# Banded attention scores in two matmul passes over stacked halves instead of three over zero-padded keys

## The reference

```python
q = q.reshape(B, nb, BLK, A_KV_HEADS, A_GROUP, A_HEAD_DIM) * (A_HEAD_DIM ** -0.5)   # 4 groups x 4 heads, 64 wide
kb = _band(k.reshape(B, S, A_KV_HEADS, A_HEAD_DIM), nb)      # keys of the blocks before, at and after
scores = jnp.einsum('bnqkgd,bnskd->bnkgqs', q, kb).astype(jnp.float32)
scores = scores - slopes * dist ; scores = where(|t-s| <= 128, scores, NEG)
p = softmax(concatenate([scores, sink]))[..., :-1]
out = jnp.einsum('bnkgqs,bnskd->bnqkgd', p, vb)
```

## Time and profile before

| | us |
|---|---|
| median of three runs | 1272.54 |
| lowest, highest | 1271.21, 1272.92 |
| span of the profiled execution (first to last instruction) | 1270.83 |
| TensorE matmuls busy | 1201.8 (95%) |
| VectorE busy | 634.5 (50%) |
| ScalarE busy | 370.1 (29%) |
| GpSimd busy | 432.6 (34%) |
| banded attention's groups: first score of g = 0, 1, 2, 3 at | 60.40, 97.33, 132.76, 168.87 |

### The profile page before, as it was taken

The page is one execution under the profiler, slowest core; times in us unless marked ns, Lnnn a source line. Parts: engine busy times, 40 slices in busy tenths (PEclk is TensorE's granted clock), DMA queues, the critical chain, the costliest instruction groups (busy, mean ns, idle before and its releaser), DMA issues.

```text
span 1270.8 us, 19309 instructions
## 1 busy us (share of the span) xinstructions
PE 1201.8 (95%) x5804; PEld 996.6 (78%) x5804; DVE 634.5 (50%) x1055; ACT 370.1 (29%) x719; POOL 432.6 (34%) x474
## 2 busy tenths in 40 slices
PE   6988899999999999999989899999999999999996
PEld 4777787878888888888967677777788888888885
DVE  6666674444432544445476767745433432343432
ACT  3167672232210011011165656532222200101101
POOL 5455543433321323334242314215333321333341
PEclk9999999999999999999999999999999999999998
DMA  6211012233333233332201001013323432333331
GB/s 158 67 35 33 17 34 67 84 99 99 90 109 98 85 98 89 106 114 88 76 18 36 19 17 33 1 34 116 99 83 99 117 93 80 92 98 99 109 90 66
DMA packets 176473, 96.62 MB, mean 76 GB/s; under 512 B 8753, under 2 KB 173105, under 8 KB 176433
## 3 DMA queue, kind: packets, MB, share of 16 engines
q1 hardware_dynamic: 176432, 96.12, 25.9%
HBM read 94.01 MB, written 2.10 MB: 76 GB/s over the span
## 4 chain that ended last, share of the span: by engine, by line
PE 78%; DVE 8%; issue 6%; POOL 3%; ACT 3%; DMA 1%; DVEq 0%; ACTq 0%; SPq 0%; POOLq 0%
PE bank L975 25%; PE bank L977 24%; PE bank L976 24%; PE bank L1419 2%; POOL w_hi L436 1%; PE bank L1116 1%; DVE stat L2010 1%; POOL bias L516 1%; DVE w_lo L1501 1%; DMA w_raw<-in_a_w_qkv 1%; DVE bpt_lo L2015 1%; DVE apt_lo L1672 0%; ACT s_b L906 0%; DVE k_dup L1592 0%; DVE w_lo L1518 0%
## 5 line engine op out<-in xcount | busy, mean ns | idle before, releaser
L1501 DVE TENSOR_TENSOR w_lo<-w_raw,w_hi 128x1024 fp32r<-128x1024 f32 (+2 forms) x151 | 202.9, 1344 | 294.5 <-POOL w_hi L436 294.4
L436 POOL TENSOR_SCALAR w_hi<-w_raw 128x1024 fp32r<-128x1024 f32 (+3 forms) x159 | 184.5, 1160 | 414.8 <-PE bank L977 404.3
L975 PE MATMUL bank<-x_hi,w_lo 128*128 128x512 f32 x784 | 309.2, 394 | 8.4 <-DVE w_lo L1501 5.3
L976 PE MATMUL bank<-x_lo,w_hi 128*128 128x512 f32 x784 | 306.9, 391 | 0.0
L977 PE MATMUL bank<-x_hi,w_hi 128*128 128x512 f32 x784 | 306.6, 391 | 0.0
L975 PEld LDWEIGHTS bank<-x_hi,w_lo 128*128 128x128 f32 x784 | 147.9, 189 | 41.6 <-DVE w_lo L1501 7.4
L977 PEld LDWEIGHTS bank<-x_hi,w_hi 128*128 128x128 f32 x784 | 148.2, 189 | 31.4
L976 PEld LDWEIGHTS bank<-x_lo,w_hi 128*128 128x128 f32 x784 | 148.2, 189 | 29.4
L975 PE MATMUL bank<-f_hi,w_lo 128*128 128x512 f32 x352 | 137.8, 391 | 1.1 <-DVE f_lo L1782 1.1
L977 PE MATMUL bank<-f_hi,w_hi 128*128 128x512 f32 x352 | 137.0, 389 | 0.0
L976 PE MATMUL bank<-f_lo,w_hi 128*128 128x512 f32 x352 | 137.0, 389 | 0.0
(11 more groups left out here) (215 smaller groups left out, 1946.9 us busy)
## 6 DMA issues: line engine op xcount, KB each, us to landing
w_raw<-in_ffn_w_gu SPq DMA_DIRECT2D x88, 512.0 KB, 3.8
w_raw<-in_ffn_w_down SPq DMA_DIRECT2D x32, 704.0 KB, 4.4
w_raw<-in_a_w_qkv SPq DMA_DIRECT2D x12, 512.0 KB, 3.7
w_raw<-in_a_w_o SPq DMA_DIRECT2D x8, 512.0 KB, 3.5
w_raw<-in_b_w_o SPq DMA_DIRECT2D x8, 512.0 KB, 3.8
w_raw<-in_b_w_in SPq DMA_DIRECT2D x4, 672.0 KB, 4.0
w_raw<-in_b_w_uq SPq DMA_DIRECT2D x4, 576.0 KB, 4.0
x_n<-in_x SPq DMA_DIRECT2D x4, 512.0 KB, 5.0
```

Of the source, the lines that this page charges most:

```text
L436: pool.tensor_scalar(split_part(w_hi, s, cols, kv), raw_part(s, cols, kv), 1.0, 1.0, ALU.mult, ALU.mult) \
L975: pe.matmul(o, ll, rh, start=start, stop=False)
L976: pe.matmul(o, lh, rl, start=False, stop=False)
L1501: dve.tensor_tensor(split_part(w_lo, s, cols, kv), raw_part(s, cols, kv), f(split_part(w_hi, s, cols, kv)), ALU.subtract) \
```

## The change

The queries are stacked instead of the keys being padded. `aq[:, hd]` has one 128-row tile for each head: the rounded query on the head's own 64 rows (0 to 63 for an even head, 64 to 127 for an odd one), and its remainder on the other 64 rows. `kp_hi` and `kp_lo` hold the group's keys twice, on both halves, with no zeros. One pass against `kp_lo` and one against `kp_hi` then sum all four partial products. The tiles that follow in memory keep their places (`k_rest` fills the room).

- PE: two matmuls for each score unit in place of three; the keys' and queries' semaphores count 1 and 4 for each group in place of 2 and 2.
- ACT: the rounding of a pair of heads (line 700) becomes two half-height operations, that of the keys (line 684) one full-height operation in place of two half-height ones.
- DVE: the remainders of a pair (line 1634) become two half-height operations that write the other half of the rows, each behind a wait of its own; the keys' remainder (line 1614) one in place of two. The zero fills of `kp_hi` and `kp_lo` at the start of the kernel (line 1559) go.

```diff
-                for b in range(2):
-                    act.activation(kp_hi[b * HD:(b + 1) * HD, b, :], k_dup[b * HD:(b + 1) * HD, g, :], ACT.Copy) \
-                        .then_inc(kp_hi_ready, 1)
+                act.activation(kp_hi[:], k_dup[:, g, :], ACT.Copy).then_inc(kp_hi_ready, 1)
...
                 wait(act, proj_free, U_Q + 2 * g + i + 1)
-                act.activation(aq_hi[:, i, :], q_tmp[:], ACT.Copy).then_inc(q_hi_ready, 1)
+                for odd in range(2):
+                    rows = slice(odd * HD, (odd + 1) * HD)
+                    act.activation(aq[rows, 2 * i + odd, :], q_tmp[rows, :], ACT.Copy).then_inc(q_hi_ready, 1)
...
-                    q = (slice(None), hd // 2, slice(n * P, (n + 1) * P))
-                    k = (slice(None), hd % 2, slice(k0 * P, (k0 + nk) * P))
-                    product(banks[u % 3][:, 0:nk * P], aq_hi[q], aq_lo[q], kp_hi[k], kp_lo[k], True, True) \
-                        .then_inc(s_done, 1)
+                    q = aq[:, hd, n * P:(n + 1) * P]
+                    k = slice(k0 * P, (k0 + nk) * P)
+                    pe.matmul(banks[u % 3][:, 0:nk * P], q, kp_lo[:, k], start=True, stop=False)
+                    pe.matmul(banks[u % 3][:, 0:nk * P], q, kp_hi[:, k], start=False, stop=True).then_inc(s_done, 1)
...
-                pe.wait_ge(kp_ready, 2 * g + 2)
-                pe.wait_ge(q_ready, 2 * g + 1)
+                pe.wait_ge(kp_ready, g + 1)
+                pe.wait_ge(q_ready, 4 * g + 2)
...
-                pe.wait_ge(q_ready, 2 * g + 2)
+                pe.wait_ge(q_ready, 4 * g + 4)
...
-            for t in (kp_hi, kp_lo, av_hi, av_lo):
+            for t in (av_hi, av_lo):
                 dve.memset(f(t[:]), 0.0).then_inc(vec_consts, 1)
...
-                for b in range(2):
-                    rows = slice(b * HD, (b + 1) * HD)
-                    wait(dve, kp_hi_ready, 2 * g + b + 1)
-                    dve.tensor_tensor(kp_lo[rows, b, :], k_dup[rows, g, :], f(kp_hi[rows, b, :]), ALU.subtract) \
-                        .then_inc(kp_ready, 1)
+                wait(dve, kp_hi_ready, g + 1)
+                dve.tensor_tensor(kp_lo[:], k_dup[:, g, :], f(kp_hi[:]), ALU.subtract).then_inc(kp_ready, 1)
...
-                wait(dve, q_hi_ready, 2 * g + i + 1)
-                dve.tensor_tensor(aq_lo[:, i, :], q_tmp[:], f(aq_hi[:, i, :]), ALU.subtract).then_inc(q_ready, 1)
+                for odd in range(2):
+                    rows, other = slice(odd * HD, (odd + 1) * HD), slice((1 - odd) * HD, (2 - odd) * HD)
+                    wait(dve, q_hi_ready, 4 * g + 2 * i + odd + 1)
+                    dve.tensor_tensor(aq[other, 2 * i + odd, :], q_tmp[rows, :], f(aq[rows, 2 * i + odd, :]),
+                                      ALU.subtract).then_inc(q_ready, 1)
```

More of the change, by code:

```diff
@@ L170, in build @@
             ("x_n", [P, NT, D], F32), ("sq0", [P, 2, T], F32), ("ss0", [P, T], F32)])
-        (q_tmp, aq_hi, aq_lo, k_dup, kp_hi, kp_lo, v_all, av_hi, av_lo, near, bias, s_a, apt_hi, apt_lo) = \
+        (q_tmp, aq, k_dup, kp_hi, kp_lo, _, v_all, av_hi, av_lo, near, bias, s_a, apt_hi, apt_lo) = \
             region(scratch, [
-                ("q_tmp", [P, T], F32), ("aq_hi", [P, 2, T], F32R), ("aq_lo", [P, 2, T], F32R),
-                ("k_dup", [P, GROUPS, T], F32), ("kp_hi", [P, 2, T], F32R), ("kp_lo", [P, 2, T], F32R),
+                ("q_tmp", [P, T], F32), ("aq", [P, HG, T], F32R),
+                ("k_dup", [P, GROUPS, T], F32), ("kp_hi", [P, T], F32R), ("kp_lo", [P, T], F32R),
+                ("k_rest", [P, 2, T], F32),
                 ("v_all", [P, NT, GROUPS * HD], F32),
@@ L498, in _ @@
             pool.wait_ge(pool_consts, 2 + HEADS)
-            pool.wait_ge(vec_consts, 6)
+            pool.wait_ge(vec_consts, 4)
             def a_group(g, last=False):
@@ L888, in _ @@
             b_q_hi(3, T_BPRE + 6)
-            act.wait_ge(vec_consts, 8)
+            act.wait_ge(vec_consts, 6)
             act.wait_ge(krope_pool, 4)
@@ L1055, in _ @@
                 k_block(k)
-            pe.wait_ge(vec_consts, 5)
+            pe.wait_ge(vec_consts, 3)
             pe.wait_ge(pt_free, KD)
@@ L1627, in a_q_out @@
                 if not (first and i == 0):
-                    wait(dve, q_ready, 2 * g + i)
+                    wait(dve, q_ready, 4 * g + 2 * i)
                 dve.scalar_tensor_tensor(q_tmp[:], banks[6 + i][:], HD ** -0.5, rs_t[:], ALU.mult, ALU.mult) \
@@ L1959, in b_k_lo @@
                 for b in range(2):
-                    wait(dve, kp_hi_ready, 2 * GROUPS + 4 * g + 2 * i + b + 1)
+                    wait(dve, kp_hi_ready, GROUPS + 4 * g + 2 * i + b + 1)
                     ins = dve.tensor_tensor(bk_lo[0:NOPE, 2 * i + b, :], banks[6 + i][b * HD:(b + 1) * HD, :],
```

## The result

The changed kernel takes 1278.67 us in the median of 7 executions (1275.49 to 1279.28), the kernel before 1272.92 (1271.14 to 1275.31) beside it. The ratio is 1.0039, 95% interval 1.0026 to 1.0052. The prediction was 1274.4 with a range up to 1277.0: the side was the one that its second rival named, the size is beyond all of its cases.

A forecast was written before the change was run, and what follows sets the result against it. The prediction took the chain over POOL, ACT and DVE, not PE, to bound most of each attention group. Borders 3 x 0.65 + 0.8 = 2.75 us added, 0.94 taken: +1.8 on 1272.5, rounded up to 1274.4; range 1270.8 to 1277.0.

The forecast's parts named there:

- What bounds the groups: Banded attention: PE bounds only the last 12.95 us of group 1; before that, a chain over POOL, ACT and DVE.
- rival 1: PE is the bound after all: all 9.3 us come off, less 2.75 at the borders, 1266 us; chance 8%.
- The savings on the chain: Unit 12 read one pass earlier per group, 0.48 us; unit 2 in group 3, 0.12; with unit 11's 0.34, 0.94 together.
- The further 0.34 for unit 11 at the low clock: Groups 0 and 2: a pass of unit 11 at clock 0.50 counts too, 0.34 us, or nothing if the clock stays up.
- ACT at the border: Borders of groups 0, 1 and 2: the second half-height rounding delays `ot_hi` and the bias, +0.65 us each group.
- DVE before group 3: Group 3: the second half-height remainder delays `ot_lo`, for which PE's output projection waits, +0.8 us, bounds 0.6 to 0.9.
- PE's wait for the second pair: Before unit 2, around 99.3 us in group 1: costs nothing, since unit 3 must wait beyond 100 anyway.
- The sum without falls: Borders add 2.75 us; the chain gives back 0.94, of which 0.34 only with the clock down in groups 0 and 2.
- The clock: Waits before unit 11 grow to about 2.4 us, PE idles more and may fall to 0.50; 25% for 1275.1 or more.
- 0.68 for a fall: Price of a clock fall in a group: group 2 with one lasted 36.11 us, group 1 without 35.43.
- the forecast's case: Borders cost more than the chain saves: 1274.4 us, itself from 1273.2 to 1275.1; chance 59%.
- rival 2: More clock falls around unit 11: one more gives +2.3 us, from the second +2.8, four +4.6 (1277); 25% for 1275.1 or more.

The follow-up runs named there:

- three medians: Changed kernel, fillers in group 0 alone: 1275.36 us; kernel before less one score pass, groups 0.92 longer: 1276.67; changed kernel, groups 0.92 longer: 1279.25.
- the fourth kernel: Changed kernel, odd half first on ACT and DVE, odd head's second rounding on POOL, no filler matmuls: 1275.14 us, ratio 1.0011.
- the two halves of the edit: Kernel before with one of three score passes left out: 1271.10 us; changed kernel with its pass against `kp_lo` made twice, so only borders differ: 1274.97.

## Right and wrong, step by step

- **What bounds the groups**: right. The part with full PE kept its 12.94 us, and 64 passes less, alone and with the clock held, are worth 0.56 us, where rival 1 wanted 9.3. The waits said so, the 95% did not.
- **The savings on the chain**: right in size, 0.56 measured for 0.60. The further 0.34 for unit 11 at the low clock rested on a fall that stays as it is; it did not.
- **ACT at the border**: the mechanism was right and the size too small. From the pair to `ot_hi` it is 0.70 for the 0.65 taken, inside the bounds. What the term had left out is that the hold goes on to the next operation: `av_hi` follows `ot_hi` after 0.41 in place of 0.28. Together 0.83, so 0.5 us more over three groups. The prediction had weighed the hold for DVE alone.
- **DVE before group 3**: right, 0.83 for 0.8. PE's wait for the second pair cost nothing, as said.
- **The sum without falls**: 2.75 - 0.60 = 2.15 by the prediction's terms; 2.7 by the profiles and 3.0 by the medians. ACT's term is 0.5 of the difference.
- **The clock**: this is the step that failed. The wait for unit 11 was expected at 2.4 us and came to 2.20; that it grows was seen, and that this side of the result hung on it too. But "0.68 for a fall" was read from groups with a fall of 3.4 us, the only kind in the attention of the trace of before, and taken as the price of any. What the forecast's case put at nothing, the 8.4 us of passes that turn into waits of PE, and rival 2 at 0.68 for each further fall, came to 4.2 us of falls by the fillers, where the kernel before had 1.2 to 1.5. The changed kernel's falls are twice as long, cost 1.5 to 1.7 each, and in the execution of the median they come in groups 0, 1 and 2; by their times nine of thirteen executions are like it. That one long fall moves the next group under the next one is not shown: three medians fit it, the profiles of those kernels support it only in part, and the fourth kernel speaks against it. The forecast's case also had no further fall at all; rival 2 had the right place and side, and even with four more falls it ended at 1277.

What stays open is what sets the point at which group 0 meets the first fall, and with it how often an execution falls into step. One or two profiles for each kernel can't tell it; the kernel with POOL's share shows that the length of the group alone doesn't decide it.

## What to carry to other kernels

Work taken from an engine that isn't the bound of its stage becomes idle time of that engine, and on PE idle time has a price of its own: before removing matmuls, look at the longest wait of PE that they lengthen and at the granted clock around it, and price a fall there as one that begins inside the wait: at this kernel's unit 11 that was twice the length and two to five times the cost of one that begins at its end or behind it (1.4 to 1.8 us for 0.3 to 0.7). In a loop whose turns last about as long as falls lie apart, a fall once met may be met again, and here the costs of the two halves of the edit didn't add up (0.7 us apart, 5.7 together); a few filler matmuls ahead of the awaited instruction are a quick test, and here took back what the falls cost. And where an operation is split by rows, let the last piece start at the row at which the next operation of that engine starts (0.26 to 0.29 us in groups 1 and 2 here).

## What the runs showed of the hardware

- The granted clock falls to 0.50 (1.2 GHz) also while PE stands idle. At unit 11 the 8 falls that began 0.6 us or more before PE went on lasted 6.8 us, the 17 that began later than that 3.4; elsewhere a fall of 6.8 us also began with PE at work (changed kernel, 661.8 us). The same wait of 2.20 us brought none, a short or a long one in different executions of one program.
- Falls in successive groups were 37.5 to 37.6 us apart (once 34.1), with the waits that they met 36.4 to 37.9 apart.
- Behind a pair of halves whose last one starts at another row, ACT's next operation came 1.32 us after the pair's start, against 1.19 where the rows were the same, and the one behind that after 0.40 against 0.26.
- POOL rounds 64x512 in 0.62 us, as fast as ACT (0.63), both reading the same tile at the same time.
